# VectorE makes the low parts of u tiles 22 to 38 between parts of the decoding; the gate matrix is stored from GpSimd's queue

## The chip, the cores and the metric

One core of a Trainium2 chip runs the whole program. The metric is the device time of one execution in microseconds. An execution that is profiled shows what each engine did: TensorE (PE) multiplies, VectorE (DVE), ScalarE (ACT) and GpSimd (POOL) work element by element, and SyncE (SP), ScalarE and GpSimd issue transfers (DMAs).

## What is computed

A transformer layer on 512 tokens of width 1024: two kinds of attention, a projection, a layer norm, then a mixture of 16384 small experts, then a second layer norm. The experts take most of the time. The reference for them, for a block of 128 tokens:

```python
s = einsum('thcd,hcnd->thcn', (xb @ w_q), sub_keys)      # 8 heads x 2 halves x 128 keys
s_top, i_top = top_k(s, 16)
cand = s_top[:, :, 0, :, None] + s_top[:, :, 1, None, :] # 256 pairs a head
best, pos = top_k(cand, 16)
eidx = take_along_axis(cand_idx, pos)                    # 16 experts a head
g = softmax(best)
h = gelu(einsum('td,thkd->thk', xb, u[eidx]))
out = einsum('thk,thkd->td', g * h, v[eidx])
```

## The kernel before

The first 128 tokens (and the 32 last ones for `u`) fetch the rows of their own experts by gathers. For the other tokens the kernel computes with all experts: 128 u tiles of 128 experts each give `h`, a matrix of gates `g` (mostly zeros) is built from the chosen indices, and 128 v tiles are multiplied by `g * h`. So the second half of the program is a sequence of 256 steps, one tile each: 96 u tiles, then u and v tiles in turn, then v tiles.

All products with weights are split in two parts, a rounded high part and the remainder (`whi`, `wlo`), which gives three matmuls for one. For each tile SyncE loads `raw` (`tile_load`), ScalarE rounds it to `whi` (`tile_high`, L970), and another engine subtracts to get `wlo` (`tile_low`): GpSimd for tiles 0 to 5 and 22 to 37 (L738), VectorE from tile 38 on (L1345); the low parts of tiles 6 to 21 have been made and stored long before and are loaded again. `wait_low` is what TensorE and SyncE wait for. There are four buffers, so a tile's low part can be made only when TensorE has left the tile four before.

Beside the first 40 tiles VectorE decodes the choice of experts. `select(n, c, part)` treats one chunk of 128 tokens (4 chunks in `SEL_ORDER`, `SEL_PARTS` = 6 parts each): top-16 of the pairs, then the indices by comparing, multiplying and summing small bf16 tensors (`ge`, `prod`, `sel`, `picks`). At its end stands `eidx` (L1470). Then VectorE goes into its loop over steps: the low part, the dot products of gathered rows (`dots_c` at the steps in `C_STEPS`, `dots` and `sums` at those in `SUM_STEPS`), the softmax weights at `NORM_STEP` (they need ScalarE's exponential of `EXP_STEP`), the transposed picks at `PICKS_STEP`, and one-hot matrices (`one_hots`, L1403 to L1409) from step 45 on.

TensorE multiplies these one-hots (`g_quad`, L1824), four tokens a quad, two quads a batch, 96 quads spread over tiles 43 to 84. ScalarE copies each quad to `stage` (`g_evac`), which has two buffers of 8 quads, a set. Twelve sets are stored to `g_scratch` in 4 transfers each (`g_store`, L629), in SyncE's queue between the tile loads (L612) and the stores of `hout` (L622). ScalarE's gelu (L991) writes `hout`, of which there are four buffers, so it waits until the store of four tiles before has landed.

GpSimd's queue has the gathers: `gather_u` (L752, two of 128 rows of 4 KB) and `gather` (L760, 128 rows of 8 KB), into a ring of `UVB` = 5 buffers, each issued as soon as VectorE has freed its buffer.

## Time and profile before

| | us |
|---|---|
| median of 3 runs | 1596.01 |
| lowest, highest | 1592.0, 1598.8 |
| the profiled execution, its own time | 1596.0 |
| its span in the trace | 1594.2 |
| TensorE busy | 1572.1 (99%) |
| VectorE busy | 1319.1 (83%) |
| ScalarE busy | 647.3 (41%) |
| GpSimd busy | 486.9 (31%) |

The span goes from the first instruction to the last; 1.8 us of the execution's time lie outside it. Matmuls are pipelined and the ends of their records are modelled, so TensorE's share of busy time says that it always had work, not that it ran at its peak. In the records, "[5.93 <-DVE wlo L1345]" behind an instruction means that its engine stood idle for 5.93 us before it, and what released it.

### The profile page before, as it was taken

How to read it: one execution, taken by the hardware profiler on the slowest of the kernel's cores; microseconds unless marked ns; L12 is line 12 of the kernel's file. 1: busy time of each engine (PE TensorE's matmuls, PEld its weight loads, DVE VectorE, ACT ScalarE, POOL GpSimd, SP SyncE). 2: the span in 40 equal slices, each digit the busy share in tenths (PEclk: the TensorE clock that was granted, in tenths of full speed). 3: DMA queues.
4: the chain of work that ended last, by engine and by line, in shares of the span. 5: the costliest groups of instructions: out<-in, count | busy, mean ns of one | idle time of the engine just before them, and what ended most of it. 6: DMA issues, size and time to landing. Idle time of an engine off the chain costs nothing.

```text
span 1594.2 us, 24556 instructions
## 1 busy us (share of the span) xinstructions
PE 1572.1 (99%) x9566; PEld 1394.9 (88%) x9566; DVE 1319.1 (83%) x2408; ACT 647.3 (41%) x1012; POOL 486.9 (31%) x243
## 2 busy tenths in 40 slices
PE   9999999999999999899999999999999999999998
PEld 8897977888989999899999999999988888888886
DVE  6564366345899999999998889999999999999997
ACT  5634355532223343345555334333333343343332
POOL 4433223352235038511010333333332332232200
PEclk9999999999999999999999999999999999999999
DMA  7872212145132998699998999999999999999971
GB/s 280 298 276 79 77 54 80 60 153 185 54 93 77 318 312 276 255 325 318 352 351 268 350 421 423 407 408 405 406 420 409 396 397 414 395 390 416 400 296 54
DMA packets 148547, 452.24 MB, mean 284 GB/s; under 512 B 12112, under 2 KB 73808, under 8 KB 127184
## 3 DMA queue, kind: packets, MB, share of 16 engines
q1 hardware_dynamic: 120528, 282.86, 49.0%
q0 software_dynamic: 23296, 151.04, 23.6%
q10 hardware_dynamic: 4608, 16.78, 2.6%
q8 instruction: 76, 1.25, 0.3%
q14 instruction: 39, 0.32, 0.0%
HBM read 395.55 MB, written 54.53 MB: 282 GB/s over the span
## 4 chain that ended last, share of the span: by engine, by line
PE 77%; DVE 18%; DMA 3%; issue 1%; ACT 1%; POOL 0%; SPq 0%; DVEq 0%; POOLq 0%; ACTq 0%
PE bank L1518 23%; PE bank L1520 23%; PE bank L1519 23%; PE bank L1824 3%; DMA h_scratch<-hout 2%; DVE idx L1259 1%; DVE idx L1251 1%; DVE val L1250 1%; DVE val L1258 1%; DVE tmp L1252 1%; DVE uvb L1363 1%; DVE wlo L1345 1%; PE bank L1660 1%; PE bank L1647 1%; PE bank L1617 1%
## 5 line engine op out<-in xcount | busy, mean ns | idle before, releaser
L1518 PE MATMUL bank<-xhi,whi 128*128 128x352 f32 (+1 forms) x1408 | 489.7, 348 | 9.8 <-DVE wlo L1345 5.9
L1520 PE MATMUL bank<-xhi,wlo 128*128 128x352 f32 (+1 forms) x1408 | 481.9, 342 | 0.0
L1519 PE MATMUL bank<-xlo,whi 128*128 128x352 f32 (+1 forms) x1408 | 481.7, 342 | 0.0
L760 POOL DMA_INDIRECT uvb<-in_uv,eidx x128 | 214.6, 1677 | 551.6 <-DVE acc L1391 405.7
L970 ACT ACTIVATE whi<-raw 128x1024 fp32r<-128x1024 f32 x220 | 231.8, 1056 | 179.5 <-PE bank L1520 156.2
L1518 PE MATMUL bank<-whi,ahi 128*128 128x512 f32 x762 | 296.6, 389 | 0.0
L1519 PE MATMUL bank<-wlo,ahi 128*128 128x512 f32 x762 | 296.5, 389 | 0.0
L1520 PE MATMUL bank<-whi,alo 128*128 128x512 f32 x762 | 296.5, 389 | 0.0
L1518 PEld LDWEIGHTS bank<-xhi,whi 128*128 128x128 f32 x1408 | 266.3, 189 | 26.8 <-DVE wlo L1345 6.2
L1519 PEld LDWEIGHTS bank<-xlo,whi 128*128 128x128 f32 x1408 | 266.8, 189 | 14.9
L1520 PEld LDWEIGHTS bank<-xhi,wlo 128*128 128x128 f32 x1408 | 266.1, 189 | 15.4
L1345 DVE TENSOR_TENSOR wlo<-raw,whi 128x1024 fp32r<-128x1024 f32 x182 | 221.8, 1220 | 44.3 <-ACT whi L970 44.1
L704 POOL TENSOR_TENSOR wlo<-raw,whi 128x2048 fp32r<-128x2048 f32 (+1 forms) x33 | 149.3, 4525 | 296.8 <-ACT whi L791 261.4
L1520 PEld LDWEIGHTS bank<-whi,alo 128*128 128x128 f32 x762 | 143.0, 188 | 29.6
L1519 PEld LDWEIGHTS bank<-wlo,ahi 128*128 128x128 f32 x762 | 143.1, 188 | 28.8
L1518 PEld LDWEIGHTS bank<-whi,ahi 128*128 128x128 f32 x762 | 143.0, 188 | 28.5
L1391 DVE SCALAR_TENSOR_TENSOR acc<-uvb,hd,acc 128x1024 f32<-128x1024 f32 x127 | 163.2, 1285 | 4.5
L991 ACT ACTIVATE hout<-bank 128x352 f32<-128x352 f32 x128 | 58.9, 460 | 234.8 <-PE bank L1520 189.6
L1353 DVE CUSTOM_DVE_ANT_0 uvb<-uvb,xn 128x1024 f32<-128x1024 f32 x128 | 151.3, 1218 | 0.0
L1013 ACT ACTIVATE ahi<-af 128x384 fp32r<-128x384 f32 x127 | 66.1, 520 | 95.5 <-DVE af L1429 95.5
L1068 DVE TENSOR_TENSOR pre_raw<-pre_raw,pre_hi 128x1024 f32<-128x1024 f32 x16 | 48.9, 3057 | 35.6 <-ACT pre_hi L857 35.5
L1436 DVE TENSOR_TENSOR alo<-af,ahi 128x384 fp32r<-128x384 f32 x127 | 69.9, 550 | 0.0
(229 smaller groups left out, 2007.3 us busy)
## 6 DMA issues: line engine op xcount, KB each, us to landing
raw<-in_u SPq DMA_DIRECT2D x118, 512.0 KB, 6.8
raw<-in_uv SPq DMA_DIRECT2D x102, 512.0 KB, 9.7
g_scratch<-stage SPq DMA_DIRECT2D x48, 512.0 KB, 6.8
gl<-g_scratch SPq DMA_DIRECT2D x32, 768.0 KB, 8.6
raw<-in_w_in SPq DMA_DIRECT2D x22, 1024.0 KB, 5.4
h_scratch<-hout SPq DMA_DIRECT2D x96, 192.0 KB, 6.1
hl<-h_scratch SPq DMA_DIRECT2D x24, 768.0 KB, 10.8
x<-in_uv SPq DMA_DIRECT2D x25, 512.0 KB
```

The costliest lines, as they stand in the source:

```text
L704: nc.gpsimd.tensor_tensor(wlo[:, s, 0:cols], raw[:, s, 0:cols], whi[:, s, 0:cols].bitcast(F32), ALU.subtract).then_inc(lo_done, 1)
L760: nc.gpsimd.indirect_dma_start(out=uvb[:, r % UVB, :], out_offset=None, in_=a["uv"][:, :], in_offset=bass.IndirectOffsetOnAxis(ap=eidx[:, ...
L970: nc.scalar.activation(hi, r, ACT.Copy).then_inc(tile_hi, 1)
L991: nc.scalar.activation(hout[:, n % 4, 0:DH], bank[6 + n % 2][:, 0:DH], ACT.Gelu).then_inc(h_gelu, 1)
L1013: nc.scalar.activation(a_bufs(t)[0], af[:, t % 4, :], ACT.Copy).then_inc(a_hi, 1)
L1345: V.tensor_tensor(lo, r, hi.bitcast(F32), ALU.subtract).then_inc(low_dve, 1)
L1353: V.tensor_tensor_reduce(out=u, in0=u, in1=xn[:, 0, :], scale=1.0, scalar=0.0, op0=ALU.mult, op1=ALU.add, accum_out=hd[:, k:k + 1]).then_i ...
L1391: V.scalar_tensor_tensor(acc[:, :], v, hd[:, k:k + 1], acc[:, :], ALU.mult, ALU.add).then_inc(sum_done, 1)
L1436: V.tensor_tensor(lo, af[:, p % 4, :], hi.bitcast(F32), ALU.subtract).then_inc(a_lo, 1)
L1518: mm(out, lh, rh, start=first, stop=False)
L1519: mm(out, lh, rl, start=False, stop=False)
L1520: return mm(out, ll, rh, start=False, stop=last)
```

## The change

The subtracts of tiles 22 to 37 go from GpSimd to VectorE. They, and tile 38's, stand now between the parts of the decoding, by the table `LOWS_IN`: behind turn 12 (the first part of the third chunk) tile 22, behind turn 14 tiles 24 and 25, and so on to tile 38 behind turn 23, the last. The loop over steps starts at 39 in place of 36. `EXP_STEP` is 37 for 36, and the first dot products `C_STEPS` stand at 39 to 44 for 37 to 43.

The stores of the gate matrix go from SyncE's queue to GpSimd's, all four of a set one behind the other at step `last + 1` (`sets_in`), where SyncE had two at `last + 2` and two at `last + 3`. GpSimd's gathers keep their order and get a place among these stores by `gather_step`; the first five wait for a tile's high part (`tile_hi`) in place of standing between subtracts.

```diff
-DVE_FIRST, DVE_LOW = 36, 38
-EXP_STEP = 36
+LOWS_IN = {12: (22,), 13: (23,), 14: (24, 25), 15: (26, 27), 16: (28, 29), 17: (30,), 18: (31,), 19: (32,), 20: (33, 34),
+           21: (35, 36), 22: (37,), 23: (38,)}
+DVE_FIRST = 39
+EXP_STEP = 37
-C_STEPS = [37, 38, 39, 40, 41, 43] + [46 + 3 * i for i in range(NCP - 6)]
+C_STEPS = [39, 40, 41, 42, 43, 44] + [46 + 3 * i for i in range(NCP - 6)]
...
+def sets_in(step):
+    for k in range(SETS):
+        last = next(t for t in range(NT) if QS * (k + 1) - 1 in quads_after(t))
+        if step == last + 1:
+            yield k
+def gather_step(r):
+    if r < UVB + NCP:
+        return C_STEPS[r - UVB] - 3
+    return SUM_STEPS[(r - UVB - NCP) // 2] - 2
...
-                for k, i in set_of_step(s):
-                    g_store(k, i)
...
+            def g_store(k, i):
+                pool.wait_ge(g_free, QS * (k + 1))
+                rows = slice(i * (NT // 4), (i + 1) * (NT // 4))
+                quads = slice(i * (NT // 16), (i + 1) * (NT // 16))
+                nc.gpsimd.dma_start(g_dram[quads, :, k, :, :].rearrange("q m n t -> m q n t"),
+                             stage[:, k % 2, rows, :].rearrange("m (q n) t -> m q n t", n=4)).then_inc(g_stored[k % 2], 16)
...
-            for s in range(PRE_END, DVE_LOW):
-                tile_low(s)
-                if s >= 24 and s % 3 == 0 and (s - 24) // 3 < UVB:
-                    gather_u((s - 24) // 3)
-            for j in range(UVB, NCP):
+            for j in range(UVB):
+                pool.wait_ge(tile_hi, PRE_END + 4 + 3 * j)
                 gather_u(j)
...
+                for k in sets_in(s):
+                    for i in range(4):
+                        g_store(k, i)
...
                 for part in range(SEL_PARTS):
                     select(n, c, part)
+                    for s in LOWS_IN.get(SEL_PARTS * n + part, ()):
+                        tile_low(s)
...
             for s in range(DVE_FIRST, 2 * NT):
-                if s >= DVE_LOW:
-                    tile_low(s)
+                tile_low(s)
```

On VectorE, in the decoding of the third chunk from its third part on, there stood before (`bposf`, `ge`, `prod`, `sel`, `jf` and `picks` are the decoding's):

```order
L1312 CAST bposf<-bpos 128x128
L1314 TENSOR_TENSOR ge<-bposf,cstb 128x1920
L1315 TENSOR_TENSOR prod<-ge,didx 128x1920
L1316 TENSOR_REDUCE sel<-prod 128x128
L1317 TENSOR_TENSOR picks<-sel,idf 128x128
L1319 TENSOR_TENSOR prod<-ge,cstb 128x1920
L1320 TENSOR_REDUCE sel<-prod 128x128
L1321 TENSOR_TENSOR jf<-bposf,sel 128x128
```

and now stands, with the subtracts as `wlo`:

```order
L1325 CAST bposf<-bpos 128x128
L1358 TENSOR_TENSOR wlo<-raw,whi 128x1024 x2
L1327 TENSOR_TENSOR ge<-bposf,cstb 128x1920
L1328 TENSOR_TENSOR prod<-ge,didx 128x1920
L1329 TENSOR_REDUCE sel<-prod 128x128
L1330 TENSOR_TENSOR picks<-sel,idf 128x128
L1358 TENSOR_TENSOR wlo<-raw,whi 128x1024 x2
L1332 TENSOR_TENSOR prod<-ge,cstb 128x1920
L1333 TENSOR_REDUCE sel<-prod 128x128
L1334 TENSOR_TENSOR jf<-bposf,sel 128x128
```

The subtracts of tiles 24, 25, 26 and 27 have come between the parts.

On GpSimd, from the copy of the indices `cidx` on, there stood before, up to the end of its subtracts:

```order
L738 TENSOR_TENSOR wlo<-raw,whi 128x1024 [waits tile_hi,cidx_in]
L738 TENSOR_TENSOR wlo<-raw,whi 128x1024 [waits tile_hi] x2
L752 DMA uvb<-in_u_rows,cidx_143 128x1024 x2
L738 TENSOR_TENSOR wlo<-raw,whi 128x1024 [waits tile_hi] x3
L752 DMA uvb<-in_u_rows,cidx_143 128x1024 x2
L738 TENSOR_TENSOR wlo<-raw,whi 128x1024 [waits tile_hi] x3
```

and now stand in the place of the last gathers of `u` rows the stores, with the gathers between them:

```order
L750 DMA uvb<-in_u_rows,cidx_143 128x1024 [waits cdot_done]
L750 DMA uvb<-in_u_rows,cidx_143 128x1024
L767 DMA g_scratch<-stage 128x8x128 [waits g_free] x4
L758 DMA uvb<-in_uv,eidx 128x2048 [waits cdot_done,idx_done]
L767 DMA g_scratch<-stage 128x8x128 [waits g_free] x4
L758 DMA uvb<-in_uv,eidx 128x2048 [waits cdot_done]
L767 DMA g_scratch<-stage 128x8x128 [waits g_free] x4
```

No subtract of these tiles is left on GpSimd, and each set of stores waits for whatever gather stands ahead of it.

On SyncE there stood before, at each set:

```order
L629 DMA g_scratch<-stage 128x8x128 [waits g_free] x2
L612 DMA raw<-in_u 128x1024 [waits low_dve]
L622 DMA h_scratch<-hout 128x384 [waits h_gelu]
L629 DMA g_scratch<-stage 128x8x128 [waits g_free] x2
L612 DMA raw<-in_u 128x1024 [waits low_dve]
```

Now its queue has the loads and the stores of `hout` alone there.

## Rows read from the trace of the kernel before

**Rows 1.** Windows: busy us (count) of PE, PEld, DVE, ACT, POOL, clock, DMA, GB/s.

```profile
650.00:700.00 50.00, 41.66 (x284) 40.81 (x283) 49.41 (x76) 18.84 (x28) 22.21 (x14) 0.93 0.79 292
900.00:950.00 50.00, 46.74 (x282) 46.22 (x281) 40.46 (x52) 17.02 (x30) 18.29 (x11) 0.97 1.03 411
1000.00:1050.00 50.00, 50.00 (x264) 45.40 (x263) 49.57 (x68) 18.47 (x32) 18.12 (x12) 1.00 1.01 410
```

**Rows 2.** Timeline of PE: start, duration, instruction, count, [idle before <-releaser].

```profile
656.11 0.66 PE L1518 MATMUL bank<-xhi,whi 128*128 128x352 f32 x1 [5.93 <-DVE wlo L1345]
...
683.05 1.09 PE L1824 MATMUL bank<-e1w,e 128*128 128x128 f16 x16
685.56 0.62 PE L1824 MATMUL bank<-e1w,e 128*128 128x128 f16 x8 [1.42 <-DVE e1w L1409]
```

**Rows 3.** Windows, just behind the wait for tile 38.

```profile
658.00:662.00 4.00, 4.00 (x15) 4.00 (x15) 4.00 (x8) 0.00 (x0) 3.39 (x3) 0.50 1.00 391
```

**Rows 4.** Waits from 500 to 950 us: total us, times, longest.

```profile
PE bank L1518 <- ACT hout L991: 3.3, 2, 2.3
PE bank L1824 <- DVE e1w L1409: 2.4, 2, 1.4
```

**Rows 5.** Timeline of ACT near 917 us.

```profile
917.54 0.46 ACT L991 ACTIVATE hout<-bank 128x352 f32<-128x352 f32 x1 [7.81 <-DMA h_scratch<-hout]
```

**Rows 6.** Timeline of DVE: chunk starts (L1285), a small addition (L1317), `eidx` (L1470).

```profile
554.49 0.28 DVE L1285 CAST idf<-idx 128x256 bf16<-128x256 uint32 x1
...
568.70 0.29 DVE L1317 TENSOR_TENSOR picks<-sel,idf 128x128 f32<-128x128 f32 x1
...
578.98 0.29 DVE L1285 CAST idf<-idx 128x256 bf16<-128x256 uint32 x1
...
594.58 3.63 DVE L1317 TENSOR_TENSOR picks<-sel,idf 128x128 f32<-128x128 f32 x1
...
623.57 0.30 DVE L1285 CAST idf<-idx 128x256 bf16<-128x256 uint32 x1
...
652.33 0.29 DVE L1470 SCALAR_TENSOR_TENSOR eidx<-picks 128x128 uint32<-128x128 f32 x1
```

**Rows 7.** Timeline of POOL, beside the third chunk.

```profile
593.27 7.20 POOL L738 TENSOR_TENSOR wlo<-raw,whi 128x1024 fp32r<-128x1024 f32 x3
```

**Rows 8.** Groups by line: count, busy us, mean ns, idle before, releaser.

```profile
L1345 DVE TENSOR_TENSOR wlo<-raw,whi 128x1024 fp32r<-128x1024 f32 x182 | 221.8, 1220 | 44.3 <-ACT whi L970 44.1
```

**Rows 9.** Timeline of ACT: gelu at each tile's end, and the table load.

```profile
642.53 0.46 ACT L991 ACTIVATE hout<-bank 128x352 f32<-128x352 f32 x1 [2.43 <-PE bank L1520]
...
646.37 0.46 ACT L991 ACTIVATE hout<-bank 128x352 f32<-128x352 f32 x1 [2.43 <-PE bank L1520]
646.73 1.05 ACT L970 ACTIVATE whi<-raw 128x1024 fp32r<-128x1024 f32 x1
647.79 1.28 ACT L1026 ACT_TABLE_LOAD   x1
```

**Rows 10.** Timeline of DVE: the end of the first one-hot batch.

```profile
682.20 0.68 DVE L1409 TENSOR_TENSOR e1w<-e1q,pickT 128x1024 f16<-128x1024 f16 x1
```

**Rows 11.** Lines of DMAs: issue ns min/median/max, first and last start.

```profile
L768 POOL DMA_DIRECT2D cidx<-cidx x4: 496/514/724, 554.9 to 556.7; - x4
...
L760 POOL DMA_INDIRECT uvb<-in_uv,eidx x128: 933/1858/1969, 762.1 to 1517.8; - x128
...
L629 SPq DMA_DIRECT2D g_scratch<-stage x48: 370/582/2649, 699.0 to 898.7; - x48
```

**Rows 12.** The page's DMA issues: count, KB each, median us to landing.

```profile
raw<-in_u SPq DMA_DIRECT2D x118, 512.0 KB, 6.8
...
g_scratch<-stage SPq DMA_DIRECT2D x48, 512.0 KB, 6.8
...
h_scratch<-hout SPq DMA_DIRECT2D x96, 192.0 KB, 6.1
```

**Rows 13.** Timeline of SyncE's queue, at the last set of stores.

```profile
893.83 2.38 SPq L629 DMA_DIRECT2D g_scratch<-stage  x2
...
900.13 5.46 SPq L612 DMA_DIRECT2D raw<-in_u  x1
```

More of the change, by code:

```diff
@@ L92 @@
 assert len(PRE_TURNS) == NPRE
-DVE_FIRST, DVE_LOW = 36, 38
-EXP_STEP = 36
+LOWS_IN = {12: (22,), 13: (23,), 14: (24, 25), 15: (26, 27), 16: (28, 29), 17: (30,), 18: (31,), 19: (32,), 20: (33, 34),
+           21: (35, 36), 22: (37,), 23: (38,)}
+DVE_FIRST = 39
+assert [s for k in sorted(LOWS_IN) for s in LOWS_IN[k]] == list(range(PRE_END, DVE_FIRST))
+EXP_STEP = 37
 NORM_STEP = 39
@@ L474, in wait_low @@
                 engine.wait_ge(lo_in[s % 4], 16 * len([t for t in range(PRE_FIRST, s + 1) if t % 4 == s % 4]))
-            elif s < DVE_LOW:
-                engine.wait_ge(low_pool, s + 1 - NPRE)
             else:
-                engine.wait_ge(low_dve, s + 1 - DVE_LOW)
+                engine.wait_ge(low_dve, s + 1 - PRE_END)
         def wait_group(engine, g):
@@ L622, in h_store @@
                 sp.dma_start(h_dram[n // 4][:, n % 4, :], hout[:, n % 4, :]).then_inc(h_stored[n % 4], 16)
-            def g_store(k, i):
-                sp.wait_ge(g_free, QS * (k + 1))
-                rows = slice(i * (NT // 4), (i + 1) * (NT // 4))
-                quads = slice(i * (NT // 16), (i + 1) * (NT // 16))
-                sp.dma_start(g_dram[quads, :, k, :, :].rearrange("q m n t -> m q n t"),
-                             stage[:, k % 2, rows, :].rearrange("m (q n) t -> m q n t", n=4)).then_inc(g_stored[k % 2], 16)
             def h_load(m):
@@ L644, in g_load @@
                 sp.dma_start(gl[:, i % 2, :, :, :], g_dram[v_tile(4 * i) // 4]).then_inc(g_in[i % 2], 16)
-            def set_of_step(s):
-                for k in range(SETS):
-                    last = next(t for t in range(NT) if QS * (k + 1) - 1 in quads_after(t))
-                    if last + 2 <= s < last + 4:
-                        yield k, 2 * (s - last - 2)
-                        yield k, 2 * (s - last - 2) + 1
             sp.wait_ge(ln_out, TC)
@@ L769, in _ @@
             pool.wait_ge(cidx_in, 16 * CG)
-            for s in range(PRE_END, DVE_LOW):
-                tile_low(s)
-                if s >= 24 and s % 3 == 0 and (s - 24) // 3 < UVB:
-                    gather_u((s - 24) // 3)
-            for j in range(UVB, NCP):
-                gather_u(j)
-            pool.wait_ge(idx_done, 1)
-            for k in range(NG):
-                gather(k)
-                if k == UVB - 1:
-                    pool.wait_ge(cdot_gelu, 1)
-                    for g in range(CG):
-                        nc.gpsimd.dma_start(ch[CP:P, g * CT:(g + 1) * CT], cgel[g * CT:(g + 1) * CT, :]).then_inc(ch_in, 16)
+            for j in range(UVB):
+                pool.wait_ge(tile_hi, PRE_END + 4 + 3 * j)
+                gather_u(j)
+            r = UVB
+            for s in range(2 * NT):
+                while r < NCP + NG and gather_step(r) <= s:
+                    if r < NCP:
+                        gather_u(r)
+                    else:
+                        if r == NCP:
+                            pool.wait_ge(idx_done, 1)
+                        gather(r - NCP)
+                    if r - NCP == UVB - 1:
+                        pool.wait_ge(cdot_gelu, 1)
+                        for g in range(CG):
+                            nc.gpsimd.dma_start(ch[CP:P, g * CT:(g + 1) * CT], cgel[g * CT:(g + 1) * CT, :]).then_inc(ch_in, 16)
+                    r += 1
+                for k in sets_in(s):
+                    for i in range(4):
+                        g_store(k, i)
         @block.scalar
```

## The prediction

> **What bounds the kernel now.** I read the stretches of 50 us first. TensorE works without a gap in nearly all of them: from 1000 to 1050 us it is busy 50.00 of 50, VectorE 49.57, and the DMA engines' share is 1.01. Two stretches lose time: 650 to 700 (41.66 busy, granted clock 0.93) and 900 to 950 (46.74 busy, clock 0.97) [rows 1]. So the bound is TensorE's own work, and the change can only win where TensorE is not at full pace. That is 50.00 - 41.66 = 8.3 us plus 0.07 x 50 = 3.5 us of clock at the first place, and 3.3 plus 0.03 x 50 = 1.5 us at the second: 16.6 us in all.
>
> The waits and the timelines name the causes. At the first place u tile 38, the first one whose low part VectorE makes at all, starts at 656.11 after a wait of 5.93 us for VectorE [rows 2]; its clock is then 0.50, the lower level of 1.2 GHz [rows 3]. 2.4 us more go to waits for the one-hots [rows 2, 4]. At the second place TensorE waits 3.3 us for ScalarE's gelu [rows 4], and ScalarE waited 7.81 us for a store of `hout` [rows 5].
>
> Why VectorE is late for tile 38 is seen in its own timeline. The decoding of one token chunk (`select`, six parts) takes 578.98 - 554.49 = 24.5 us for the second chunk. The third takes 623.57 - 578.98 = 44.6 us and the fourth 652.33 - 623.57 = 28.8 us, for the same instructions [rows 6]. A small addition that took 0.29 us takes 3.63 us at 594.58; it ends at 598.21, where the second of GpSimd's three subtracts (7.20 us from 593.27, so 2.40 each) has ended [rows 6, 7]. The excess is 20.1 + 4.3 = 24.4 us. The Trainium skill (SBUF — State Buffer, Who interferes with whom) says that a VectorE instruction with two SBUF inputs and a GpSimd instruction that reads SBUF shut each other out for a whole instruction; this trace agrees, by those rows.
>
> **Part 1, the subtracts.** GpSimd loses 16 subtracts (tiles 22 to 37); nobody waited for GpSimd there, so the saving is only the 24.4 us of VectorE's held-up decoding. VectorE gains them and now makes 17 (22 to 38) before the decoding ends. One takes 1.22 us [rows 8], 1.14 when packed between others; at 1.18 that is 20.1 us. The indices `eidx` come at 652.3 - 24.4 + 20.1 = 648.0.
>
> Do the tiles come in time? TensorE's pace is 646.37 - 642.53 = 3.84 us a tile [rows 9], and tile 38 could start at 656.11 - 5.93 = 650.2. From the part lengths of the second chunk each low part is ready 3.4 to 8 us ahead of its tile; the last, tile 38, at about 648, 2 us ahead. So the wait of 5.93 us goes. The error of this margin is small: if a subtract cost 1.3 us, 17 of them would bring 2 us and tile 38 would start on time to the microsecond.
>
> What is late next is the first one-hot batch, which TensorE needs behind tile 43. Before, VectorE needed 682.88 - 652.33 = 30.6 us from `eidx` to its end [rows 6, 10]. Tile 38's subtract has left this stretch (-1.2). But the weights there need ScalarE's exponential, which now stands behind the gelu of tile 37 (end of that tile 650.2, then 0.5 gelu, 1.05 high part, 1.28 table load [rows 9], about 0.6 for itself: 653.6), while VectorE is there at 651.8: +1.8. So the batch is ready at 648.0 + 30.6 - 1.2 + 1.8 = 679.2. TensorE arrives at 650.2 + 6 x 3.84 + 1.15 for the transposed picks = 674.4 and waits 4.8 us. It passed this point at 683.05 before [rows 2]. Gain 3.9 us. The wait can bring the clock down once more as the one of 5.93 us did; of that 0.5 to 2 us stay, since the next two batches are VectorE-bound as before. I take 1.0. **Sum of part 1: -2.9 us** (bounds -3.9 and -1.9).
>
> **Part 2, the stores leave SyncE's queue.** 48 stores of 512 KB in 512-byte rows [rows 11, 12] no longer stand between the loads of tiles and the stores of `hout`. SyncE's queue was held there: 5.46 us for one load at 900.13, behind the last four stores from 893.83 on [rows 13]. This is what made ScalarE wait 7.81 us. So up to 3.3 + 1.5 = 4.8 us can go. Against it: in this stretch the DMA engines are full (share 1.03, 411 GB/s [rows 1]), and two tiles ask for 2 x 512 + 2 x 192 KB [rows 12] and two gathers of 1 MB in 7.7 us, some 450 GB/s. The bytes stay. What SyncE's transfers win, the gathers lose, and they feed VectorE. I take half: **-2.4 us** (bounds 0 and -4.8).
>
> **Part 3, the stores enter GpSimd's queue.** No row shows a plain GpSimd DMA of 1024 rows. The nearest is the copy of `cidx`, 32 rows in 0.50 us; the gathers of 128 rows take 0.93 us when undisturbed and 1.86 at the median [rows 11]. If rows cost nothing, one store costs 0.5 us. A straight line through 0.50 and 0.93 gives 0.0045 us a row and 5.0 us; in proportion to the gather it is 7.5 us. I take 2 us, nearer to the plain row: it is the same kind of instruction, and the gather reads an index per row besides, which the doubling of its median beside VectorE points to. With 2 us a set of four costs 8 us of a set's 17.7 us ((893.83 - 699.0) / 11 [rows 11, 13]), and it hides behind TensorE: two `stage` buffers, four banks. The Trainium skill (DMA: Bandwidth & Descriptors, Anatomy of one DMA) says that many descriptors can be put out before their extra cost shows; no run here shows that yet, and by it this part is nothing. The last set stands between gathers 24 and 25 and holds them by about 3 us; VectorE's lead over TensorE is there about three tiles, 11 us, so it costs nothing.
>
> Also moved: the 11 later gathers of `u` rows wait in the same order with the stores; their buffers are used 15 steps later. SyncE's waits for the last stores at step 94 come some 10 us after these. `C_STEPS` and `EXP_STEP` move by one or two steps and are in the count above.
>
> **Sum.** -2.9 - 2.4 = -5.3 us. The profiled run's span is 1594.2 and its time 1596.0, equal to the median of the runs (1596.01), so the forecast is 1596.0 - 5.3 = 1590.7, said as 1590.5.
>
> **Rivals.**
> A, **GpSimd becomes the bound** (slower). Place: the twelve sets between 700 and 900 us. At 5.0 us a store a set takes 4 x 5.0 + 1.9 of gathers = 21.9 us against 17.7. `stage` comes free late, ScalarE stands before the next set, then TensorE. Price: (21.9 - 17.7) x 11 = 46, less some 8 us that banks and leads take up = 38, less 2.9 of part 1 (nothing of part 2 is left to win): 1631. At 7.5 us: 1741. It decides from 4t + 1.9 = 17.7, t = 4.0 us. For it: the line through the two rows, and 1024 rows is eight times the largest DMA that GpSimd issues now. Against it: the kinds differ. The Trainium skill (SBUF — State Buffer, Summary: rules for kernel authors) advises against DMAs from GpSimd's queue beside VectorE's faster copy modes; the gathers' median of 1.86 us bears it out in part, and by it this rival is the likelier. Chance 0.25.
>
> B, **given back**: the DMA engines' fullness or gathers held behind the last set stop VectorE near 915 us, or the margin of 2 us at tile 38 is too thin. Then part 1's 2.9 stays at most: 1593 to 1600, say 1595. VectorE at 49.57 of 50 from 1000 on [rows 1] has little to make up with. Chance 0.22.
>
> C, **all of it**: no clock loss at the new wait and the second place clean, 3.9 + 4.8 = 8.7: 1587, with a chance of 0.16.
>
> My forecast (1588 to 1593) has 0.37.
>
> **How the numbers follow.** About 0.5%, 8 us, is what a measurement of this kernel can tell from no change. Faster by more (under 1588) is C and the edge of the forecast: 0.25. Slower by more (over 1604) is A: 0.26. Between: 0.49. The range goes from 1585 to 1631; above it lies A with a dearer store (0.1), below it little.
>
> **What the profile after would show.** Right: GpSimd has no subtract beside the decoding; third and fourth chunk take about 34 us each, all small additions near 0.3 us; no wait at tile 38; a wait of about 5 us for the one-hots before the first quad; stores near 2 us each on GpSimd; no 7.8 us wait of ScalarE near 917. Wrong: stores over 4 us with GpSimd busy from 700 to 900 and ScalarE waiting for `g_scratch` (A); a wait of VectorE for a gather near 915 (B); low parts late for tiles 37 or 38.

## The result, and the profile after

The changed kernel takes 1598.16 us (median of 20 runs, 1595.59 to 1601.44) where the kernel before takes 1592.52 us beside it (median of 20, 1589.45 to 1600.68). The ratio is 1.0029, with an interval of 1.0020 to 1.0038; like every ratio below it compares all executions of both kernels and is not the quotient of the two medians. I had said 1590.5: the change costs 0.3% where I saw a gain of 0.3%. What follows reads the profiled execution, whose span is 1598.1 us against 1594.2.

The stretches that answer to [rows 1], same columns:

```profile
650.00:700.00 50.00, 44.00 (x314) 43.09 (x313) 46.94 (x75) 21.90 (x32) 21.80 (x15) 0.93 0.89 317
900.00:950.00 50.00, 39.83 (x246) 39.01 (x244) 34.96 (x43) 13.32 (x23) 18.54 (x11) 0.98 1.02 412
950.00:1000.00 50.00, 49.65 (x259) 46.16 (x260) 48.10 (x66) 21.00 (x36) 17.74 (x11) 0.95 0.99 387
```

The first place is better (44.00 busy for 41.66). The second is far worse (39.83 for 46.74), and the clock falls behind it, in the next 50 us (0.95; the kernel before had 49.51 busy and 1.00 there).

**The first place.** The timeline of VectorE, with the starts of the third and fourth chunk (L1298), the small addition of each (L1330) and `eidx` (L1485), answers to [rows 6]; below it the first quad of one-hots in TensorE's timeline, which answers to the second row of [rows 2]:

```profile
579.27 0.29 DVE L1298 CAST idf<-idx 128x256 bf16<-128x256 uint32 x1
...
598.09 0.29 DVE L1330 TENSOR_TENSOR picks<-sel,idf 128x128 f32<-128x128 f32 x1
...
614.03 0.28 DVE L1298 CAST idf<-idx 128x256 bf16<-128x256 uint32 x1
...
647.62 0.28 DVE L1485 SCALAR_TENSOR_TENSOR eidx<-picks 128x128 uint32<-128x128 f32 x1
```

```profile
679.81 1.86 PE L1838 MATMUL bank<-e1w,e 128*128 128x128 f16 x16 [5.33 <-DVE e1w L1422]
```

The chunks take 34.8 and 33.6 us, the addition 0.29 us for 3.63, `eidx` comes at 647.62 (I had said 648.0). Tile 38 has no wait. The first quad starts at 679.81, 3.24 us earlier than before, behind a wait of 5.33 us.

**The stores.** The line of the gate stores on GpSimd, its columns as in [rows 11], and the page's line on packets, of the kernel before and then of the changed one:

```profile
L767 POOL DMA_DIRECT2D g_scratch<-stage x48: 885/902/979, 701.6 to 899.5; - x48
```

```profile
DMA packets 148547, 452.24 MB, mean 284 GB/s; under 512 B 12112, under 2 KB 73808, under 8 KB 127184
```

```profile
DMA packets 105538, 452.23 MB, mean 283 GB/s; under 512 B 12112, under 2 KB 24656, under 8 KB 84176
```

The page's line on GpSimd's own queue (packets, MB, share of the DMA engines), before and after:

```profile
q0 software_dynamic: 23296, 151.04, 23.6%
```

```profile
q0 software_dynamic: 30208, 176.21, 28.2%
```

A store of 1024 rows of 512 bytes costs GpSimd 0.90 us, less than half of the 2 us that I took. The same bytes now travel in 43,000 fewer packets. The 48 stores add 30,208 - 23,296 = 6,912 packets to GpSimd's queue, 144 a store. In all, 49,152 packets of under 2 KB are gone, which is 1,024 for each store, and 6,144 of 2 to 8 KB have come, 128 for each: GpSimd's queue joins the short rows, SyncE's did not. From 700 to 900 us TensorE is busy without a gap.

**The second place.** The chain of work that ended last, from 900 us on: start, duration, what.

```profile
901.45 17.84 DMA uvb<-in_uv,eidx
919.30 1.23 DVE uvb L1366
...
925.56 0.33 SPq L628
925.93 23.73 DMA h_scratch<-hout
949.75 0.47 ACT hout L1004
950.35 0.63 PE bank L1532
```

And GpSimd's timeline ahead of it, then the line of waits of TensorE from 890 to 1000 us:

```profile
895.06 1.69 POOL L758 DMA_INDIRECT uvb<-in_uv,eidx  x1 [0.30 <-issue]
896.75 3.63 POOL L767 DMA_DIRECT2D g_scratch<-stage  x4
901.45 1.93 POOL L758 DMA_INDIRECT uvb<-in_uv,eidx  x1 [1.07 <-DVE acc L1404]
```

```profile
PE bank L1532 <- ACT hout L1004: 10.5, 3, 6.8
```

The four stores of the last set are issued in 3.63 us, as they should be, but 2 MB now stand in GpSimd's queue in front of the next gather. That gather lands 17.84 us after the start of its issue. VectorE waits 6.85 us for it:

```profile
919.30 1.23 DVE L1366 CUSTOM_DVE_ANT_0 uvb<-uvb,xn 128x1024 f32<-128x1024 f32 x1 [6.85 <-DMA uvb<-in_uv,eidx]
920.46 0.08 DVE L1366 DVE_READ_ACCUMULATOR2_ANT hd<- 128x1 f32 x1
920.46 1.22 DVE L1358 TENSOR_TENSOR wlo<-raw,whi 128x1024 fp32r<-128x1024 f32 x1
```

VectorE's wait reaches TensorE in two ways. The short one goes through ScalarE's program, in which the small gelu of VectorE's dot products stands ahead of that of `hout`:

```profile
920.57 0.20 ACT L1019 ACTIVATE hgel<-hd 128x2 f32<-128x2 f32 x1 [6.69 <-DVE hd L1366]
```

TensorE waits 1.2 us for ScalarE right behind it. The long one goes through SyncE's queue: behind VectorE's waiting instruction stands a low part (920.46), behind that the load of a tile, and behind that, in the same queue, the stores of `hout`. One of them (192 KB, issued at 925.93) takes 23.73 us. ScalarE waits 9.5 us for it and TensorE 6.8 us for ScalarE. In all TensorE waits 10.5 us at this place, where it was 3.7 before. It never waits for a low part: VectorE's lead covers those, and those only.

The sum of the two profiles: -3.2 us at the first quad; at the second place idle time and clock loss are (50.00 - 39.83) + 0.02 x 50 + (50.00 - 49.65) + 0.05 x 50 = 14.0 us for 3.3 + 1.5 + 0.5 = 5.3 before. That makes +5.5 for a difference of 3.9 between the spans; a clock digit of 0.01 is 0.5 us in such a row, which is as near as this sum gets.

### The profile page after: what moved, and what is told of

It is laid out like the page before. It is cut to its first block, busy times and chain, and to the rows that moved or that the text cites. A ratio compares the mean times of both kernels' runs of the same rounds, so it can differ in the third digit from the quotient of the medians.

```text
span 1598.1 us, 24568 instructions
## 1 busy us (share of the span) xinstructions
PE 1571.6 (98%) x9566; PEld 1394.3 (87%) x9566; DVE 1308.4 (82%) x2424; ACT 650.2 (41%) x1012; POOL 489.8 (31%) x275
## 2 busy tenths in 40 slices
DMA packets 105538, 452.23 MB, mean 283 GB/s; under 512 B 12112, under 2 KB 24656, under 8 KB 84176
## 3 DMA queue, kind: packets, MB, share of 16 engines
q0 software_dynamic: 30208, 176.21, 28.2%
## 4 chain that ended last, share of the span: by engine, by line
PE 87%; DVE 7%; DMA 4%; issue 1%; ACT 1%; POOL 0%; SPq 0%; DVEq 0%; POOLq 0%; ACTq 0%
PE bank L1532 27%; PE bank L1533 26%; PE bank L1534 26%; PE bank L1838 3%; DVE wlo L1358 2%; DMA h_scratch<-hout 1%; DMA uvb<-in_uv,eidx 1%; PE bank L1771 1%; DVE uvb L1376 1%; PE bank L1674 1%; PE bank L1661 1%; PE bank L1631 1%; PE bank L1647 1%; DMA qraw<-in_w_q 1%; PE bank L1620 0%
## 5 line engine op out<-in xcount | busy, mean ns | idle before, releaser
L1532 PE MATMUL bank<-xhi,whi 128*128 128x352 f32 (+1 forms) x1408 | 489.0, 347 | 10.8 <-ACT hout L1004 10.5
L1358 DVE TENSOR_TENSOR wlo<-raw,whi 128x1024 fp32r<-128x1024 f32 x198 | 241.1, 1220 | 37.7 <-ACT whi L983 37.2
L750 POOL DMA_INDIRECT uvb<-in_u_rows,cidx x32 | 44.0, 1374 | 135.2 <-ACT whi L983 65.8
L1081 DVE TENSOR_TENSOR pre_raw<-pre_raw,pre_hi 128x1024 f32<-128x1024 f32 x16 | 44.7, 2792 | 39.2 <-ACT pre_hi L870 39.2
```

The source lines that it names most:

```text
L1358: V.tensor_tensor(lo, r, hi.bitcast(F32), ALU.subtract).then_inc(low_dve, 1)
L1532: mm(out, lh, rh, start=first, stop=False)
```

## Experiments: which part costs

The theories. **Q**: the loss comes from the queue in which the last set of stores stands. **E**: it comes from part 1, which brings everything 3.4 us earlier to a place where the DMA engines are full. Each time stands beside that of the kernel before on the same chip. The diffs leave out what only moves along: the definitions of `g_store` and `set_of_step` and the counts of the semaphores.

**Part 1 alone** (stores back in SyncE's queue; `after` is the changed kernel):

```diff
 SyncE, step s of after:
+                for k, i in set_of_step(s):
+                    g_store(k, i)
 GpSimd:
-                for k in sets_in(s):
-                    for i in range(4):
-                        g_store(k, i)
```

> The changed kernel with the gate stores back in SyncE's queue, where the kernel before had them: only the subtracts, the order of the u gathers and the two step numbers stay changed. Theory Q (the loss at 900 to 960 us comes from the queue: the last set's 2 MB stand in GpSimd's queue ahead of the gathers, and VectorE waited 6.9 us for one of them): the loss goes and part 1's gain of about 3 us stays, so 1592.5 - 2.9 = 1589.6, ratio to before 0.998, and VectorE has no wait for a gather near 912 us. Theory E (the loss comes because part 1 brings everything 3.4 us earlier to the place where the DMA engines are full, whatever queue the stores take): the loss stays without the queue's change, ratio 1.001 to 1.003, and TensorE waits some 10 us for hout between 920 and 955 us.

Measured: 1594.11 us, the kernel before 1595.4; ratio 1.0011 (0.9994 to 1.0029). TensorE waits 4.4 us for `hout` there, not 10.5, and VectorE has no wait for a gather at all. Its row for the second place:

```profile
900.00:950.00 50.00, 45.64 (x275) 45.12 (x274) 39.71 (x50) 16.15 (x27) 19.44 (x11) 0.97 1.03 410
```

The loss has gone back to about the size that it had before (46.74 busy). That is what Q expects. But the 2.9 us of part 1 don't show in the times; this is taken up below.

**Part 2 alone** (the kernel before, with the loop of the changed kernel that issues gathers and stores on GpSimd, and SyncE's stores taken out):

```diff
 GpSimd, behind the subtracts of tiles 22 to 37 of before:
-            for j in range(UVB, NCP):
-                gather_u(j)
-            ...
+            for s in range(2 * NT):
+                while r < NCP + NG and gather_step(r) <= s:
+                    ...
+                for k in sets_in(s):
+                    for i in range(4):
+                        g_store(k, i)
```

> The kernel before with the gate stores issued by GpSimd, as the changed kernel does, and no other edit: the subtracts stay on GpSimd, tile 38's wait stays. Theory Q: part 1's 3 us are missing and the whole loss of 8.8 us at the second place is there: 1592.5 + 8.8 = 1601, ratio 1.004 to 1.006. Theory E: the stores' place costs nothing or gives up to 2.4 us, ratio 0.998 to 1.000. The wait of VectorE for a gather after the last set (6.9 us in the changed kernel) should be there by Q, not by E.

Measured: 1601.61 us against 1595.4; ratio 1.0041 (1.0018 to 1.0064). The chain of work shows the same pair as in the changed kernel, a gather behind the stores and a slow store of `hout`:

```profile
905.35 16.69 DMA uvb<-in_uv,eidx
...
928.69 22.70 DMA h_scratch<-hout
```

So the stores' new place costs 6.2 us by the medians, without part 1. E falls.

**The last set alone in SyncE's queue**, eleven sets on GpSimd:

```diff
 SyncE:
+                for k, i in set_of_step(s):
+                    if k == SETS - 1:
+                        g_store(k, i)
 GpSimd:
                 for k in sets_in(s):
+                    if k == SETS - 1:
+                        continue
```

> The changed kernel with only the last of the twelve sets of gate stores in SyncE's queue; eleven sets stay on GpSimd. Theory Q in its narrow form (the last set is the only one that meets the gathers): as good as with all stores in SyncE's queue, 1589.6, ratio 0.998, with ScalarE's wait for a store of hout near 915 us back. Rival Q2 (the loss comes from all the stores' larger packets or from gathers of u rows held behind earlier sets): stays near the changed kernel, 1.002 to 1.003. Theory E: 1.001 to 1.003 too, then told from Q2 by the run with part 1 alone.

Measured: 1593.58 us, ratio 1.0002 (0.9985 to 1.0020), the same as part 1 alone. VectorE's wait for gathers from 890 to 960 us is this one line (total, times, longest):

```profile
DVE uvb L1389 <- DMA uvb<-in_uv,eidx: 0.3, 1, 0.3
```

Eleven of the twelve sets cost nothing in GpSimd's queue; the twelfth makes the whole loss. It is the only one that falls where a pair of gathers of 1 MB each is asked for every two tiles (the pairs start at 882 us, the set before is issued at 870).

**The last set's bytes out of the way.** The same number of bytes leaves some 27 us earlier, behind the stores of the tenth set and from its buffer. The kernel leaves out the last set's own gates, so its output is not the layer's; it is there for the time alone:

```diff
                 for k in sets_in(s):
+                    if k == SETS - 1:
+                        continue
                     for i in range(4):
                         g_store(k, i)
+                    if k == SETS - 3:
+                        for i in range(4):
+                            g_store(k, i, k + 2)
```

> The changed kernel, but the last set's four stores go out some 27 us earlier, behind the stores of set 9 and from its stage buffer: the same bytes and the same places in memory, the wrong gates in the last set. What it tells is what 2 MB of stores cost when they stand beside the first gathers. Theory Q: VectorE's wait for a gather goes, and as 2 MB (some 5 us of full DMA engines) are gone from the full stretch, the rest of the loss as well: 1586 to 1588, ratio 0.996 to 0.997. Theory E (start of gathers 3.4 us earlier on full engines) would keep half or more of the loss: above 1592. If the early place only moves the trouble, ScalarE waits for g_scratch at set 11 and TensorE for it.

Measured: 1591.55 us, ratio 0.9985 (0.9964 to 1.0006). VectorE has no wait for a gather, and TensorE's wait for `hout` is 3.1 us. It gives back 6.6 us of the changed kernel's time, not 10 to 12: without these 2 MB 3.1 us of idle time and 1.5 us of clock stay at 900 to 950 us, and a store of `hout` issued at 923.04 still takes 21.05 us. So that place loses time even without the stores.

**The last set in four pieces**, one ahead of each of the next four gathers:

```diff
+SPREAD = (9, 10, 11, 12)
                 while r < NCP + NG and gather_step(r) <= s:
+                    if r - NCP in SPREAD:
+                        g_store(SETS - 1, SPREAD.index(r - NCP))
...
                 for k in sets_in(s):
+                    if k == SETS - 1:
+                        continue
```

> The changed kernel with the last set's four stores not in a row, but one ahead of each of the next four gathers in GpSimd's queue; the same bytes in the same queue. If what costs is 2 MB in a row ahead of one gather, VectorE's wait of 6.9 us shrinks to some 2 us and the time falls by 4 to 8 us, 1590 to 1594. If what costs is that the bytes stand in the gathers' queue at all (full engines, the gathers together get the same share), the wait is only cut into pieces and the time stays within 2 us of 1598.

Measured: 1598.23 us, the kernel before 1592.34; ratio 1.0037 (1.0023 to 1.0052). Not a microsecond is won. VectorE's wait is cut into pieces:

```profile
DVE uvb L1371 <- DMA uvb<-in_uv,eidx: 5.0, 3, 2.7
```

But its chain of work no longer goes through a gather:

```profile
912.79 13.95 DMA g_scratch<-stage
...
927.66 23.27 DMA h_scratch<-hout
```

The last piece is issued only at 912.79 and takes 13.95 us, and SyncE stands 7.8 us for it at the load of gates of step 94, with a tile's load and a store of `hout` behind it. In the changed kernel SyncE has no such wait. So this run made one delay smaller and brought in another; it doesn't show whether 2 MB in pieces cost the gathers less than 2 MB in a row.

**The load of gates later:**

```diff
-GL_FIRST, GL_SECOND = 94, 98
+GL_FIRST, GL_SECOND = 96, 98
```

> The changed kernel with the first load of gates (768 KB, waiting for all gate stores) at step 96 instead of 94. The chain of the changed kernel goes through a store of hout of 192 KB that takes 23.73 us from 925.93 us on, right behind this load in SyncE's queue (issued 922.61). If the load ahead of it is the cause, that store falls to 15 us or less and TensorE's wait of 6.84 us at 950 goes: 1590 to 1593. If the cause is VectorE's wait for the gather before it (everything late behind it comes at once) and full DMA engines, the time stays within 2 us of 1598: the bytes stay.

Measured: 1596.20 us, the kernel before 1591.77; ratio 1.0026 (1.0007 to 1.0045). TensorE's waits for `hout` are 5.7 us in four pieces instead of 10.5 in three, and yet a later store of `hout` takes 20.69 us. By the medians the load's place in SyncE's queue is worth some 2 us, less than the 5 to 8 us that it should have been as the cause. VectorE's wait for the gather is still there (7.2 us). Why a store of 192 KB takes 20 to 24 us there isn't shown further than this; in the kernel before, one issued at 908.78 took 15.28 us, and the median of all is 6.1 [rows 12].

## Experiments: full DMA engines

Up to step 97 a pair of gathers is asked for every two tiles. With a tile, a store of `hout` and a gather of 1 MB in 3.84 us this is an estimated 450 GB/s, and the engines move 411 to 423 from 900 to 1000 us of the kernel before. Two pairs fewer there, two more behind step 156:

```diff
-SUM_STEPS = [85, 87, 89, 91, 93, 95] + [97 + i * 59 // 27 for i in range(27)] + [156 + i * 94 // 31 for i in range(31)]
+SUM_STEPS = [85, 88, 91, 94] + [97 + i * 59 // 27 for i in range(27)] + [156 + i * 93 // 33 for i in range(33)]
```

In the changed kernel:

> The changed kernel with four instead of six gather pairs before step 97 (steps 85, 88, 91, 94) and the two missing pairs in the stretch from step 156 on. Between 908 and 950 us the DMA engines are full at some 420 GB/s while 1.7 MB a tile of 3.84 us, some 450 GB/s, are asked for. Theory Q with its condition (the queue in which the last set stands costs time only because the engines are full there): with 1.36 MB a tile, 355 GB/s, both the 6.9 us wait of VectorE and most of the 10.5 us of TensorE's waits for hout go; 1598.2 - 8 to 12 = 1586 to 1590, ratio 0.995 to 0.998. Rival O (order alone: a gather behind 2 MB in its queue comes late however empty the engines are): VectorE still waits 5 us or more once near 915 us and the time stays above 1594. Rival V: VectorE, 0.99 busy from 1000 us on, can't take what was put off and the loss comes back at the end of the kernel.

In part 1 alone:

> The same spacing of the gather pairs with all gate stores in SyncE's queue (part 1 of the change alone). If the queue matters only where the engines are full, this is within 2 us of the spaced kernel with the stores on GpSimd, 1586 to 1590. If the stores' place in a queue costs by itself (rival O), this one is faster than the other by 5 us or more.

In the kernel before:

> The kernel before with the same spacing and nothing else. It should gain what it lost at 900 to 950 us, up to 4.8 us: some 1590 by the median of this chip (1595.4), and part 1 then is worth the difference to the spaced kernel with part 1, 2 to 3 us. If the two groups of times of the kernel before (near 1587 and near 1595.5) come from that stretch, this kernel has one group only, near 1588 to 1590. If they come from the clock at tile 38, both groups stay.

Measured, the kernel before 1592.34 us beside all three:

| kernel, with spaced gathers | median us | ratio (interval) | wait of TensorE for `hout` |
|---|---|---|---|
| changed (stores on GpSimd) | 1586.71 | 0.9967 (0.9955 to 0.9978) | none |
| part 1 alone (stores on SyncE) | 1586.91 | 0.9965 (0.9953 to 0.9978) | none |
| before | 1585.10 | 0.9960 (0.9947 to 0.9973) | none |

The second place of the changed kernel is then clean:

```profile
900.00:950.00 50.00, 50.00 (x314) 50.00 (x314) 40.52 (x52) 19.97 (x33) 14.58 (x11) 1.00 1.02 412
```

GpSimd issues the last set's four stores ahead of a gather there too, and VectorE doesn't wait:

```profile
891.17 3.62 POOL L767 DMA_DIRECT2D g_scratch<-stage  x4 [4.95 <-ACT stage L1013]
898.11 1.92 POOL L758 DMA_INDIRECT uvb<-in_uv,eidx  x1 [3.32 <-DVE acc L1404]
```

In this schedule the queue of the stores makes no difference (1586.71 and 1586.91). Rival O, that a gather behind 2 MB comes late however empty the engines are, is weakened but not excluded: the spacing asks less of the engines, it gives each gather three tiles in place of two, and it lets the stores out 5.6 us earlier (891.17 for 896.75), because no pair of gathers that waits for a buffer stands ahead of them. No run separates these three. The DMA share is still 1.02: a full share alone doesn't tell whether somebody waits.

But the third row was a surprise. With the second place clean, the kernel **without** part 1 should have been 3 us slower than those with it, and it is 1.7 us faster.

## Experiments: what part 1 is worth

The times of that third kernel lie in two groups: nine of twelve from 1584.2 to 1585.8, three from 1589.3 to 1589.9. The two kernels with part 1 have one group each (1586.2 to 1587.7, 1586.0 to 1588.1). The profiled execution of the third was in the lower group (1585.76). Its timelines of GpSimd, VectorE and TensorE, which answer to [rows 7], [rows 6] and [rows 2]:

```profile
589.04 1.02 POOL L752 DMA_INDIRECT uvb<-in_u_rows,cidx  x1
590.37 1.69 POOL L752 DMA_INDIRECT uvb<-in_u_rows,cidx  x1 [0.30 <-issue]
592.08 5.18 POOL L738 TENSOR_TENSOR wlo<-raw,whi 128x1024 fp32r<-128x1024 f32 x2
598.00 2.60 POOL L738 TENSOR_TENSOR wlo<-raw,whi 128x1024 fp32r<-128x1024 f32 x1 [0.73 <-ACT whi L970]
```

```profile
594.71 0.29 DVE L1317 TENSOR_TENSOR picks<-sel,idf 128x128 f32<-128x128 f32 x1
...
609.27 0.29 DVE L1285 CAST idf<-idx 128x256 bf16<-128x256 uint32 x1
...
646.89 0.29 DVE L1470 SCALAR_TENSOR_TENSOR eidx<-picks 128x128 uint32<-128x128 f32 x1
```

```profile
650.67 0.43 PE L1518 MATMUL bank<-xhi,whi 128*128 128x352 f32 x1 [0.43 <-DVE wlo L1345]
```

Up to here it is the code of the kernel before, and yet the third chunk takes 30.1 us, not 44.6, `eidx` comes at 646.89, not 652.33, and tile 38 waits 0.43 us, not 5.93. **Theory S**: the subtracts hold VectorE by an amount that depends on how they fall beside the decoding, and it differs from execution to execution. The next runs test it, together with the seam: `HOT0` moves the one-hot batches to later tiles.

```diff
-HOT0, HOT1, HOT2 = 45, 83, 87
+HOT0, HOT1, HOT2 = 47, 83, 87
```

With both parts of the change and spaced gathers:

> The spaced kernel with both parts of the change (1586.7), with the one-hot batches starting two tiles later (HOT0 47 for 45; the 44 dense batches then in 36 steps for 38). It tests what the seam still costs: there TensorE waits 5.3 and 0.7 us for the first one-hots and loses 3.5 us of clock, 9.5 us in all. TensorE has two more u tiles (7.7 us) to do before it needs them, and VectorE one or two subtracts of 1.2 us more ahead of them: the wait goes and with it the clock loss if that comes from the wait, 1577 to 1581. If the clock falls whatever TensorE waits for, 1581 to 1583. Against it: a set now takes 16.8 us for 17.7, and if VectorE (about 0.9 busy at 800 to 900 us) can't keep it, the wait comes back later and nothing is won.

The same with `HOT0` 46:

> The same with one tile (HOT0 46). The wait of 5.3 us shrinks by 3.84 less 1.2, to some 2.7 us: 1582 to 1584; the clock loss of 3.5 us stays if a short wait is enough for it.

The kernel before, spaced gathers, `HOT0` 47:

> The kernel before with spaced gathers (1585.1, with times near 1584.7 and near 1589.7) and HOT0 47. Theory S (the subtract's place matters: GpSimd's subtracts hold VectorE by an amount that depends on how they fall beside the decoding, and tile 38's wait is 0.4 us in one execution and 5.9 in another): two groups of times stay, the lower one as fast as the kernel with part 1 and HOT0 47, the upper one 4 to 5 us slower, because that wait stands ahead of the one-hots and isn't covered by their later start. If part 1 is worth nothing beyond its own wait for the one-hots, the medians are equal; if it is worth 3 us once the next stall is away, this kernel is slower than e9 by 1 to 5 us.

The kernel before, unchanged:

> The kernel before once more, for one more profile. Its times lie in two groups, near 1587 to 1590 and near 1595. By theory S a profile of the lower group shows tile 38's wait under 1 us and eidx at 647, one of the upper group a wait near 5.9 us and eidx at 652; the stretch from 900 to 950 us loses TensorE some 3 to 5 us in both. If the wait is near 5.9 us in an execution of the lower group, theory S falls.

Measured: 1584.93 us (ratio 0.9952, 0.9929 to 0.9976), 1587.15 us (0.9977, 0.9958 to 0.9995), 1579.49 us (0.9948, 0.9923 to 0.9972) and 1597.94 us (one execution); the kernel before has 1589.93 beside them. The first two are slower than expected; the reason comes below. The third has two groups as S says, and wider apart than expected: seven of twelve from 1578.8 to 1579.8, five from 1586.8 to 1588.7. Its profiled execution was in the upper group (1586.79), with these rows of GpSimd, VectorE and TensorE:

```profile
589.17 3.01 POOL L752 DMA_INDIRECT uvb<-in_u_rows,cidx  x1 [0.16 <-issue]
```

```profile
652.41 0.29 DVE L1470 SCALAR_TENSOR_TENSOR eidx<-picks 128x128 uint32<-128x128 f32 x1
```

```profile
656.19 0.66 PE L1518 MATMUL bank<-xhi,whi 128*128 128x352 f32 x1 [5.38 <-DVE wlo L1345]
```

The kernel before once more (1597.94 us) has a wait of 5.38 us at tile 38 and `eidx` at 653.44. For the lower group:

> The kernel before with spaced gathers and HOT0 47 once more, for a profile of its lower group of times (seven of twelve executions near 1579, five near 1588). By theory S an execution of the lower group has a wait of TensorE at tile 38 under 1 us, eidx near 647 and the third chunk of the decoding near 30 us; one of the upper group has 5.4 us, 652 and 43 to 45 us, as every profile above 1585 us so far. A time near 1579 with the long wait would throw the theory out.

Measured: 1578.81 us, as S had said of such a time: TensorE has no wait at tile 38 at all, and the third chunk takes 31.0 us. GpSimd's gather and VectorE's `eidx`:

```profile
589.56 1.03 POOL L752 DMA_INDIRECT uvb<-in_u_rows,cidx  x1 [0.16 <-issue]
```

```profile
643.24 0.29 DVE L1470 SCALAR_TENSOR_TENSOR eidx<-picks 128x128 uint32<-128x128 f32 x1
```

So S has stood a test that it could have failed: six profiled executions have GpSimd's subtracts in the old order, four with a wait of 5.4 to 5.9 us and two with 0 and 0.4, and two executions of the very same code (`HOT0` 47) are 8.0 us apart. In all four with the long wait the first gather of `u` rows took 3.00 or 3.01 us, in both others 1.02 or 1.03. These two are not free of the excess either. Third and fourth chunk together take 67.7 and 64.1 us, where two chunks of the second's length would be 49.0; that is 18.7 and 15.1 us, for the 24.4 of the prediction. Is this gather the cause? Two runs move it (kernel before, spaced, `HOT0` 47):

```diff
-                if s >= 24 and s % 3 == 0 and (s - 24) // 3 < UVB:
-                    gather_u((s - 24) // 3)
+                if s >= 25 and s % 3 == 1 and (s - 25) // 3 < UVB:
+                    gather_u((s - 25) // 3)
```

> The same kernel with GpSimd's first five u gathers one subtract later (behind tiles 25, 28, 31, 34, 37 for 24, 27, 30, 33, 36). In the slow profiles the first gather took 3.01 us beside the decoding and the three subtracts behind it ran in a row (7.20 us); in the fast one it took 1.02 us. If the two groups come from where the gather falls beside VectorE's copies, the share of the two groups changes or one goes, while the two levels stay near 1579 and 1587. If the groups come from something else (the clock, the DMA engines), seven to five stays.

```diff
-                if s >= 24 and s % 3 == 0 and (s - 24) // 3 < UVB:
-                    gather_u((s - 24) // 3)
-            for j in range(UVB, NCP):
+            for j in range(NCP):
                 gather_u(j)
```

> The same kernel with no gather between GpSimd's subtracts: all of them behind tile 37's. Without the 3 us gather the subtracts can no longer fall behind and run in a row, so theory S with the gather as its cause expects one group, at 1579, if the first gathers (from 641 us) land in time for the dots at step 37. If each subtract alone is enough to push VectorE into the long form, both groups or only the upper one (1587) stay.

Measured: 1584.84 us (ratio 0.9967, 0.9956 to 0.9978; six from 1583.0 to 1585.0, one 1589.7) and 1585.19 us (0.9963, 0.9950 to 0.9976; 1582.2 to 1586.8), the kernel before 1590.43. Neither level of the old order stays, which neither expectation had. In the last, `eidx` is there at 640.63, earlier than in any other profile (chunks of 30.5 and 31.0 us), but the gathers come late and VectorE stands 7.3 us for one: 41.81 us busy from 600 to 650. So where the gathers fall changes how long VectorE is held, and an excess of some 12 us stays with no gather between the subtracts. That the first gather alone sets it is likely but not shown: moving it also moved the four others.

**The exponential one step earlier** (both parts, spaced, `HOT0` 47). In the first profile of that kernel VectorE stood for ScalarE's exponential:

```profile
654.38 0.55 DVE L1349 TENSOR_REDUCE hsum<-picks 128x24 f32<-128x384 f32 x1 [3.31 <-ACT picks L1039]
```

```diff
-EXP_STEP = 37
+EXP_STEP = 36
```

> Both parts of the change, spaced gathers, HOT0 47 (1584.9), with ScalarE's exponential one step earlier (EXP_STEP 36, as in the kernel before). VectorE stood 3.31 us for it at 651 us, and TensorE waits 2.0 and 1.5 us for the one-hots behind that. The exponential then stands ahead of tile 37's gelu, some 648.6 to 650.5 us: VectorE's wait shrinks by 2 to 3.3 us and 1.5 to 3 us come back: 1582 to 1583.5. If TensorE waits for that gelu instead, nothing comes back.

Once more:

> Both parts of the change with spaced gathers, HOT0 47 and EXP_STEP 36 once more, since the first time had six executions and one of them of double length: 1579.5 to 1580.1 again, one group, ratio 0.992 to 0.995.

Measured: 1579.72 us (ratio 0.9935, 0.9922 to 0.9947; the kernel before 1590.43; five executions from 1579.5 to 1580.1 and one of 3166.8, twice the length, which is left out) and 1580.06 us (0.9914, 0.9886 to 0.9941; 1579.7 to 1580.9; the kernel before 1591.77). Against 1584.93 that is 4.9 to 5.2 us, not 1.5 to 3, over runs on three chips. The stretch 650 to 700 us without and with the edit:

```profile
650.00:700.00 50.00, 46.53 (x313) 45.85 (x313) 46.17 (x72) 21.05 (x30) 24.93 (x16) 0.93 0.90 334
```

```profile
650.00:700.00 50.00, 48.61 (x357) 47.92 (x356) 49.45 (x76) 21.70 (x33) 28.27 (x20) 1.00 0.96 352
```

2.1 us are busy time of TensorE, and 3.5 us are clock: with waits of 3.5 us in all (the longest 2.0) it was 0.93 in this stretch, with 1.7 us (the longest 1.4) it was 1.00. The waits alone don't settle it: the kernel whose gathers stand one subtract later lost more busy time in the same stretch (the longest wait 2.2 us) and kept 1.00:

```profile
650.00:700.00 50.00, 45.34 (x320) 43.93 (x319) 47.78 (x73) 20.51 (x31) 25.07 (x16) 1.00 0.88 326
```

The kernel with the earlier exponential beats both the changed one (by 18 us) and the one before (by 11 us). It does not beat the kernel before with the same spacing and the same `HOT0`, whose lower group lies at 1578.8 to 1579.8. What it has over that one is that all of its times lie in one group, as far as eleven executions tell.

`HOT0` 46 gained nothing because I had forgotten an entry of `C_STEPS`: step 46 brings two dots of 1.14 us for the class token ahead of the batch, so VectorE has 1.2 + 2.3 us more to do for a start that TensorE reaches 3.84 us later. The batch's last one-hots began at 682.82 us, where they had begun at 678.93 with `HOT0` 45.

## Why the prediction was wrong, point by point

**The bound and the two places** were right: what the change moved, it moved there.

**Part 1, inside one execution,** was right nearly to the row: `eidx` 647.62 (said 648.0), chunks of 34 us, no wait at tile 38, a wait of 5.33 us (said 4.8), first quad 679.81 (said 679.2 for its one-hots). The clock loss stayed at 3.5 us as a digit of 0.93. **What failed is what it was compared with.** The term of 24.4 us for VectorE's excess, and with it the wait of 5.93 us at tile 38, came from one execution of the kernel before and was taken for the kernel's. It is there in only a part of the executions. In the kernels with spaced gathers, part 1 gives 1586.8 against 1584.8 in nine executions of twelve and 1589.7 in three: +2.0 or -2.9. The second is my number, for the kind of execution that I had read; no profile was taken of an execution of that group. The sum shows where the other sign comes from. The 17 subtracts cost what I had said (third and fourth chunk together 68.4 us for 49.0, so 19.4 for 20.1), but what they take away was only 18.7 and 15.1 us in the two profiles with a short wait or none, and then nothing is won. By the medians part 1 costs 1.7 us there, and with `HOT0` 47 it costs 5.4 (1584.93 against 1579.49), until the exponential goes to its old step.

That the exponential behind tile 37's gelu would cost 1.8 us was also a term that was too small: VectorE stood 2.47 us for it in the spaced kernel and 3.31 with `HOT0` 47, and the clock went with it; setting it back was worth 5 us.

**Part 2** failed. "What SyncE's transfers win, the gathers lose" was the right sentence, but I took half of SyncE's loss as a gain and bounded it by 0 below. Nothing in the rows excluded a loss; that the gathers feed VectorE, and that behind VectorE's waiting instruction stand the low part, the tile's load and the stores of `hout`, was the reason to expect one. The place measured +8.7 us in the profile, for parts 2 and 3 together, not -2.4.

**Part 3** was wrong in both of its numbers, in opposite ways. A store costs 0.90 us for the 2 us taken, and rival A, GpSimd as the bound, falls. I had counted rows. The store's 1024 rows leave in 128 packets of 2 to 8 KB, and the 0.90 us are close to the 0.93 of a gather of 128 rows; that the packets and not the rows set the issue time fits this, but no run shows it by itself. The Trainium skill (DMA: Bandwidth & Descriptors, Anatomy of one DMA) says that many descriptors can be put out before their extra cost shows. This trace agrees by rows, 0.90 us for 1024 and some 0.5 for 32 [rows 11]; what a store of 1024 separate packets would cost GpSimd, no run here shows.

"Holds them by about 3 us" counted only the time that GpSimd needs to issue the last set. The 2 MB themselves stand in front of the gather: it landed after 17.84 us, where the kernel before shows 10.4 us at the median from 890 to 915 us. VectorE stood 6.85 us for it. "VectorE's lead over TensorE is there about three tiles, 11 us, so it costs nothing" was the second error: the lead protects the low parts, and TensorE indeed never waited for one. It doesn't protect ScalarE, which stood 6.69 us for VectorE's dot products, nor SyncE's queue, where the next tile's load and the stores of `hout` stood behind VectorE's low part. The step that failed is this term of 0: the issue was priced and the transfer wasn't, and the lead was taken to cover all who wait for VectorE. With the last set alone back in SyncE's queue the time was 1593.58 (ratio 1.0002), with all in GpSimd's 1598.16 (1.0029).

**Rival B** is what happened, at the place and with the sign that its first mechanism names: gathers held behind the last set stop VectorE near 915 us (912.4 to 919.3), time 1593 to 1600. I gave it 0.22.

## What to carry to other kernels

Where a transfer goes into another engine's DMA queue, price its bytes in that queue, not only its issue: here 2 MB ahead of a gather cost it some 7 us, and the gather's consumer had less than that in hand. Then ask of everyone who waits for that consumer, not only of the engine that bounds the kernel. Thinning out the crowded stretch gave more than the choice of the queue (two gather pairs moved gave 7 to 11 us), and behind it that choice made no difference.

A gain computed from a stall in one profiled execution needs a second profile of the same kernel. Two groups of times of the kernel before were a hint; a stall that two engines make together need not be there next time.

## What the runs showed of the hardware

- GpSimd's queue joins rows of 512 bytes: 48 stores of 512 KB took 49,000 packets fewer under 2 KB (73,808 to 24,656) and 43,000 fewer in all than from SyncE's queue. A store of 1024 such rows held GpSimd for 0.90 us, a gather of 128 rows for 0.93 when undisturbed.
- A gather behind 2 MB of stores in GpSimd's queue took 17.84 us to land, and 16.69 in the kernel with part 2 alone; the median of the kernel before was 10.4 at that place.
- The same code beside the same decoding took one of two courses in six profiled executions: a gather issue of 1.0 or of 3.0 us at 589 to 590 us, a chunk of 30 to 31 or of 43 to 45 us, and in two executions of one kernel 8 us of its time.
- The granted clock of the stretch from 650 to 700 us was 0.93 with a longest wait of 2.0 us in it, and 1.00 with one of 1.4 us and, in another kernel, with one of 2.2 us.
- A DMA share of 1.02 stood both where VectorE waited 6.9 us for a gather and where nobody waited at all.
